# A three-block transformer on one core: row norms as fp32r products with ones, a T sum moved behind the output projection, and one whole block pair per feed-forward layer

## The chip, the core and the metric

The kernel runs on one core of one Trainium2 chip. The metric is the device time of one execution in microseconds (us), the median over several executions. The matmuls are done on TensorE (PE), elementwise work on VectorE (DVE), activations and copies on ScalarE (ACT), some additions and accumulating DMAs on GpSimd (POOL), and weight loads are issued by SyncE (SP).

## What is computed

The input is a sequence of 512 tokens of width 1024, in float32. Three layers follow each other. Each has a mixing part (mLSTM, banded attention, and a differential plus forgetting attention), an output projection that is added to x, and a feed-forward part. What matters here is the norms and the feed-forward part:

```
def rmsnorm(x, g):
    y = x * rsqrt(mean(x * x, axis=-1) + EPS)
    return y * g

def conv_ffn(h, w_up, conv_w, conv_b, w_down):   # layers 0 and 1
    u, g = split(h @ w_up)                       # 1024 -> 2 x 2816
    g = causal_dwconv(g, conv_w, conv_b)         # 3 taps along the tokens
    return (silu(g) * u) @ w_down

# layer 2 (second block): the same without the convolution, EPS 1e-5
# between layers 1 and 2: x = rmsnorm(rmsnorm(x, final_g), norm1_g_2) feeds the projections
```

## The kernel before

**Layout.** x lies in SBUF as X, transposed: 8 tiles k of 128 channels by 512 tokens. Every product is made of fp32r (a rounded float32) parts: an operand is split into a high part (H, by an ACT copy) and a low part (L, by a DVE subtraction), and three matmuls (WH with H, WH with L, WL with H) replace one. A group of 24 matmuls (8 k-steps of three) of 512 columns makes one tile of 128 outputs by 512 tokens.

**Order.** `order()` writes out one list of steps by hand. Each engine's function (`tensor`, `scalar`, `vector`, `gpsimd`) walks this one list and issues its own part of each step, so that each engine's queue is in the order of the list, and an instruction that waits holds up everything behind it on its engine. Semaphores connect the engines (`mark` and `at`). `conv_ahead` puts the weight splits (`conv` and `cconv`: WH by ACT at L1933 and L1944, WL by DVE at L2458 and L2480) as early as a slot of the four half-size weight slots is free.

**Norms.** Weights are applied to the unnormed x times g; the factor 1/rms of a token multiplies the result. The squares of X are summed into acc by POOL (L3183) or DVE. For `ffn0`, `ffn1`, `n2` and `kv` the steps `rstd_first` and `rstd_second` follow: PE sums acc over the partitions with 4 fp32 matmuls of one column (L1348), ACT takes the root of 128x4 values (L2082), DVE the inverse (L2662), PE spreads these with 4 fp32 matmuls of 128 columns (L1354), and ACT copies the spread rows to Rsb (L2103). The norm between layers 1 and 2 (`join_first`, `join_second`, `join_third`) does it for acc and for a second sum acc2.

**Feed-forward (`ffn_wino`).** 11 pairs of blocks of 256 hidden channels (gate and up). The first WHOLE[i] pairs, (2, 2, 1) for layers 0, 1 and 2, are done plainly: 4 tiles g, g, u, u of 24 matmuls each of 512 columns (L1460). The others use a Strassen-Winograd scheme, `wp`: 7 products of 24 matmuls each of 256 columns (L1793), PE's order q1, q5, q6, q3, q7, q2, q4, each with its own weight chunk of 128x1024, four of which are sums of blocks made by DVE (`wsum`, L2474). q1 and q6 share a PSUM bank: q6 waits until ACT has copied q1 out (`wcopy`, L2010). The products need sums of x as moving operands, the T sums: for each of four pairs p of k-tiles `wtB` (ACT, L1951), `wtS` (four DVE operations L2492 to L2503, then an ACT copy L1957 to TH) and `wtL` (DVE, L2510, to TL). In between stand the pieces of the down projection (`wd`, L1819), which are added to X by accumulating DMAs, and at the end its tail (`wtail`, L1842).

**Around the change.** Of the output projection, `out_rest` makes the tiles m = 0 to 7; after tile m the step `res_norm` adds it to X (DVE, L2917), makes hH of tile m (ACT, L2268), its square (ACT, L2276) and hL of tile m-1 (DVE, L2425); `res_last` makes hL of tile 7. `T_SUMS` names the T sums that stand behind an output tile: p = 0 behind tiles 4 and 5, and `wtB` of p = 1 behind tile 5. Where WHOLE is 1, `conv_ahead` (the chunks of q6 and q3), `wt0` twice (the conv taps on DVE, L2536, and silu on ACT, L1981; in layer 2 silu alone), `wy0`, then q1 with its `wcopy` stand in this order behind the last u tile. In layer 1 `fence acc2`, `gg` and `gate_weights C` stand between `res_last` and the first g tile: both ACT and DVE wait there for POOL's last square sum, and DVE waits for a small load.

Of the kernel before, what the change touches and what calls it, by code (L numbers as in the profile page):

```python
# [34 lines left out]
WHOLE = (2, 2, 1)  # L35
# [4 lines left out]
T_SUMS = {4: (("wtB", 0), ("wtS", 0)), 5: (("wtL", 0), ("wtB", 1))}  # L40
# [280 lines left out]
def pieces(hd):  # L321
# [3 lines left out]
    if hd % 2 == 0:  # L325
# [11 lines left out]
             "C": ([4, 5, 0, 1, 2, 3, 6, 7], 6)}  # L337
NEXT_NORM = {"A": "ffn0", "B": "ffn1", "C": "n2"}
# [8 lines left out]
def order():  # L347
# [5 lines left out]
    def put(*x):  # L353
        steps.append(x)
# [60 lines left out]
    def tile_done(*x):  # L415
# [13 lines left out]
        if norms:  # L429
            step = norms.pop(0)  # L430
            if step:
                put(*step)
                if step[0] == "join_second":
                    deferred.append(("join_third",))
# [154 lines left out]
    def ffn_wino(i, end):  # L589
# [404 lines left out]
def program(nc, wall, xt, memt, colsd, biasd, consts, rope, gatew, out):  # L994
    ctx = ExitStack()
    with ctx:
# [28 lines left out]
        K = place("K", [128, 5, 128])  # L1025
        KB = place("KB", [128, 3, 128], BF16)
        acc = place("acc", [128, 512])
        sq = [place(f"sq{i}", [128, 512]) for i in range(2)]
        diag = place("diag", [128, 512])
        held_w = place("held3", [128, 2, 256], offset=top[0] - 2048)  # L1030
# [108 lines left out]
        Tf = place("Tf", [128, 4, 256], offset=wino + 49152)  # L1139

# [169 lines left out]

        def normed(st, k):

            return ("hH", st, k), ("hL", st, k)
# [5 lines left out]
        def tensor(e):  # L1319
# [31 lines left out]

            def spread_column(o, c):

                return e.matmul(o, small[:, c:c + 1].broadcast_to([128, 128]), ident, start=True, stop=True)  # L1354

            def spread(what, b, before, key, c0=4):

                w.wait_ge(*at("rcol", "n1" if what == "join" else what))
# [19 lines left out]
            for what, *a in STEPS:  # L1378
# [85 lines left out]

                elif what == "tm":
# [73 lines left out]
                elif what == "rstd_rows":  # L1539
# [4 lines left out]
                    w.wait_ge(*at("acc" + SQ_LAST[a[0]], a[0], 7))  # L1544
                    e.matmul(ps[b][:, :], ones, acc[:, :], start=True, stop=True).then_inc(*mark("sums", a[0]))
# [5 lines left out]
                elif what == "join_first":  # L1551
                    b, before = bank(("rs", "join"), ("jsq", 0))
                    if before:
                        w.wait_ge(*at(*before))
                    w.wait_ge(*at("accD", "n1", 7))
                    sums(b, acc, 0, ("sums", "n1"))
                    w.wait_ge(*at("acc2", 7))
                    sums(b, acc2, 4, ("sums", "join"))

                elif what == "join_second":  # L1560
                    b, before = bank(("R", "n1"), ("Rsb", "n1"))
                    spread("n1", b, before, ("spread", "n1"))

                elif what == "join_third":
                    b, before = bank(("R", "join"), ("Rsb", "join"))
                    spread("join", b, before, ("spread", "join"), 32)
# [339 lines left out]
        def scalar(e):  # L1906
            w, mark = Lane(e), partial(ev.mark, "act")

            for what, *a in STEPS:
# [175 lines left out]
                elif what == "rstd_rows":  # L2085
# [7 lines left out]
                elif what == "last_sums":  # L2093
# [3 lines left out]
                                 bias=small[:, 61:62], scale=1.0 / 1024).then_inc(*mark("rsq", "last", h))  # L2097

# [249 lines left out]
                elif what == "join_first":  # L2348
                    w.wait_ge(*at("sums", "join"))
                    e.activation(small[:, 0:4], ps[BANK[("rs", "join")]][:, 0:4], ACT.Sqrt, bias=small[:, 60:61],  # L2350
                                 scale=1.0 / 1024).then_inc(*mark("rsq", "n1"))
                    w.wait_ge(*at("jsq", 1))
                    e.activation(small[:, 44:48], small[:, 40:44], ACT.Sqrt, bias=small[:, 61:62]).then_inc(
                        *mark("rsq", "join"))

                elif what == "join_second":
                    w.wait_ge(*at("spread", "n1"))
                    for x in R_USED["n1"]:
                        w.wait_ge(*at(*x))
                    e.activation(Rsb[:, :], ps[BANK[("R", "n1")]][:, :], ACT.Copy).then_inc(*mark("Rsb", "n1"))  # L2360

                elif what == "join_third":
                    w.wait_ge(*at("spread", "join"))
                    e.activation(acc2[:, :], ps[BANK[("R", "join")]][:, :], ACT.Copy).then_inc(*mark("Rsb", "join"))
# [17 lines left out]

                elif what == "lam_later":
                    w.wait_ge(*at("lamS"))
                    e.activation(small[:, 10:12], ps[BANK["lam"]][:, 0:2], ACT.Exp).then_inc(*mark("lamE"))
# [28 lines left out]
        def vector(e):  # L2414
# [8 lines left out]
            def low_part(st, k, g):  # L2423
# [3 lines left out]
                                       op1=ALU.subtract).then_inc(*mark("hL", st, k))  # L2427

# [13 lines left out]
            for what, *a in STEPS:  # L2442
# [76 lines left out]
                elif what == "wg0":  # L2519
# [3 lines left out]
                    w.wait_ge(*at("Rsb", FFN_NORM[i]))  # L2523
# [53 lines left out]
                elif what == "wgr":  # L2577
                    i, st = a
                    w.wait_ge(*at("Rsb", FFN_NORM[i]))
# [96 lines left out]
                elif what == "join_first":  # L2676
# [12 lines left out]
                    for x in RCOL_USED["n1"]:  # L2689
                        w.wait_ge(*at(*x))  # L2690
# [745 lines left out]
```

## Time and profile before

| | |
|---|---|
| three runs | 1775.87, 1775.97, 1776.04 us, median 1775.97 |
| profiled execution, own time | 1776.19 us |
| its span, first to last instruction | 1774.4 us |
| granted TensorE clock, mean | 0.999 |
| PE busy | 99% |
| DVE, ACT, POOL busy | 72%, 53%, 12% |

The profile is of one execution. The own time holds 1.8 us beside the span. In a timeline a row has start, duration, engine, line, operation, and in brackets how long its engine was idle before it and what released it; rows overlap a little, since an instruction begins before the one before it has ended. In the chain of work that ended last, a row has start, duration, engine and line of a piece.

### The profile page before, as it was taken

Reading aid. Unit: us, or ns where it says so; the run is one execution under the profiler, and the core shown is the slowest. Engines: PE = TensorE matmul, PEld = TensorE weight load, DVE = VectorE, ACT = ScalarE, POOL = GpSimd, SP = SyncE. Lnnn points to the kernel's source line nnn. Section 1 sums busy time; section 2 is a strip of 40 time slices with the busy share of each in tenths; the row PEclk is TensorE's granted clock in tenths of the full one; section 3 lists DMA queues with packets and bytes.
Section 4 is the critical chain, followed back from the end, with each engine's and each line's share of the span. In section 5 each row is a group of like instructions: output and inputs, shape, how many; then the busy total and the mean of one; then the engine's idle time right before and its main releaser. Section 6 shows DMA issues by size and latency. Waiting matters only on the chain.

```text
span 1774.4 us, 26361 instructions
## 1 busy us (share of the span) xinstructions
PE 1764.7 (99%) x10750; PEld 1533.1 (86%) x10750; DVE 1273.1 (72%) x1772; ACT 949.1 (53%) x1439; POOL 205.8 (12%) x225
## 2 busy tenths in 40 slices
PE   9999999999999999999999999999999999999998
PEld 7877788999999887777899999978777899999997
DVE  6878567788786655656888787687767487766766
ACT  6645444655555544755565555552567455454454
POOL 0001220110111200002011110103001101111110
PEclk9999999999999999999999999999999999999999
DMA  6231223654545343212364554443221235555442
GB/s 249 72 95 61 71 95 107 154 137 137 143 121 141 88 147 110 96 48 87 106 169 117 155 128 140 111 119 106 73 96 48 97 106 144 142 140 145 108 134 81
DMA packets 61623, 205.19 MB, mean 116 GB/s; under 512 B 7344, under 2 KB 9520, under 8 KB 53184
## 3 DMA queue, kind: packets, MB, share of 16 engines
q1 hardware_dynamic: 38832, 162.55, 27.7%
q0 software_dynamic: 17280, 31.46, 10.0%
q10 hardware_dynamic: 5392, 9.51, 1.7%
q8 instruction: 85, 1.39, 0.3%
q14 instruction: 34, 0.28, 0.0%
HBM read 169.38 MB, written 2.13 MB: 97 GB/s over the span
## 4 chain that ended last, share of the span: by engine, by line
PE 96%; DVE 2%; ACT 1%; DMA 0%; issue 0%; DVEq 0%; SPq 0%; ACTq 0%
PE ps L1793 31%; PE ps L1460 21%; PE ps L1819 16%; PE ps L1374 7%; PE ps L1479 4%; PE ps L1842 2%; PE ps L1499 2%; PE ps L1606 2%; PE ps L1651 2%; PE ps L1631 2%; PE ps L1690 1%; PE ps L1671 1%; PE ps L1860 1%; PE ps L1423 1%; DVE WL L2458 0%; PE ps L1354 0%
## 5 line engine op out<-in xcount | busy, mean ns | idle before, releaser
L1793 PE MATMUL ps<-hH,WL 128*128 128x256 f32 x896 | 253.6, 283 | 0.0
L1793 PE MATMUL ps<-hL,WH 128*128 128x256 f32 x896 | 253.6, 283 | 0.0
L1793 PE MATMUL ps<-hH,WH 128*128 128x256 f32 x896 | 253.4, 283 | 0.0
L2480 DVE TENSOR_TENSOR WL<-raw,WH 128x1024 fp32r<-128x1024 f32 x138 | 168.1, 1220 | 116.9 <-ACT WH L1944 116.9
L2458 DVE TENSOR_TENSOR WL<-raw,WH 128x1024 fp32r<-128x1024 f32 (+1 forms) x137 | 166.9, 1257 | 92.1 <-ACT WH L1933 91.8
L1460 PE MATMUL ps<-hH,WH 128*128 128x512 f32 x544 | 215.3, 396 | 0.0
L1460 PE MATMUL ps<-hH,WL 128*128 128x512 f32 x544 | 211.9, 390 | 0.0
L1460 PE MATMUL ps<-hL,WH 128*128 128x512 f32 x544 | 211.9, 390 | 0.0
L3207 POOL DMA_DIRECT2D X<-sq x120 | 104.8, 962 | 862.1 <-ACT sq L1999 860.2
L1793 PE MATMUL ps<-TH,WL 128*128 128x256 f32 x672 | 190.2, 283 | 0.0
L1793 PE MATMUL ps<-TL,WH 128*128 128x256 f32 x672 | 190.2, 283 | 0.0
L1793 PE MATMUL ps<-TH,WH 128*128 128x256 f32 x672 | 190.1, 283 | 0.0
L2480 DVE TENSOR_TENSOR WL<-Wsum,WH 128x1024 fp32r<-128x1024 f32 x112 | 136.7, 1221 | 69.2 <-ACT WH L1944 69.1
L1933 ACT ACTIVATE WH<-raw 128x1024 fp32r<-128x1024 f32 (+1 forms) x137 | 134.4, 1028 | 88.9 <-PE ps L1460 44.9
L1793 PEld LDWEIGHTS ps<-hL,WH 128*128 128x128 f32 x896 | 171.9, 192 | 1.2
L1793 PEld LDWEIGHTS ps<-hH,WH 128*128 128x128 f32 x896 | 171.9, 192 | 1.2
L1793 PEld LDWEIGHTS ps<-hH,WL 128*128 128x128 f32 x896 | 171.9, 192 | 0.0
L1819 PE MATMUL ps<-FH,WH 128*128 128x512 f32 x432 | 168.7, 391 | 0.0
L1819 PE MATMUL ps<-FL,WH 128*128 128x512 f32 x432 | 168.7, 390 | 0.0
L1819 PE MATMUL ps<-FH,WL 128*128 128x512 f32 x432 | 168.0, 389 | 0.0
L1944 ACT ACTIVATE WH<-raw 128x1024 fp32r<-128x1024 f32 x138 | 144.7, 1053 | 24.9 <-PE ps L1793 18.4
L1944 ACT ACTIVATE WH<-Wsum 128x1024 fp32r<-128x1024 f32 x112 | 118.0, 1054 | 55.9 <-PE ps L1793 42.6
(420 smaller groups left out, 3865.3 us busy)
## 6 DMA issues: line engine op xcount, KB each, us to landing
raw<-in_wall SPq DMA_DIRECT2D x166, 512.0 KB, 4.3
raw<-in_wall SPq DMA_DIRECT2D x65, 1024.0 KB, 4.9
X<-sq POOLq DMA_DIRECT2D x120, 256.0 KB, 4.0
bias<-in_bias ACTq DMA_DIRECT2D x12, 256.0 KB, 2.9
raw<-in_wall SPq DMA_DIRECT2D x8, 256.0 KB, 6.9
X<-in_xt SPq DMA_DIRECT2D x8, 256.0 KB, 7.7
CB<-rows ACTq DMA_DIRECT2D x8, 256.0 KB, 3.4
out_y<-X SPq DMA_DIRECT2D x8, 256.0 KB, 2.2
```

The lines of the kernel that those rows point to most:

```text
L1374: mm = e.matmul(ps[b][:, :], ww[:, k, c:c + 128], x, start=(k == seq[0] and i == 0), stop=(k == seq[-1] and i == 2))
L1460: mm = e.matmul(ps[b][:, 0:N], ww[:, k, c:c + 128], x[:, k, 0:N], start=(k == 0 and i == 0), stop=(k == 7 and i == 2))
L1479: mm = e.matmul(o, x[:, k, t * 128:t * 128 + 128], ww[:, k, :], start=(k == 0 and i == 0), stop=(k == 7 and i == 2))
L1499: mm = e.matmul(ps[b][:, :], x[:, k, t * 128:t * 128 + 128], ww[:, kx, :], start=(k == 0 and i == 0), stop=(k == 7 and i == 2))
L1606: mm = e.matmul(ps[b][:, c:c + L], queries[u["kind"]][r, u["m"], t * 128:t * 128 + 128], keys[u["kind"]][r, u["m"], 0:L], start=opens, sto ...
L1793: mm = e.matmul(ps[b][:, 256 * u:256 * u + 256], ww[:, p, 128 * u:128 * u + 128], x, start=(opens and p == 0 and u == 0 and n == 0), stop= ...
L1819: mm = e.matmul(ps[BANK["wd", i, g, m]][:, :], ww[:, kx, mi * 128:mi * 128 + 128], x[:, f % 8, :], start=(kx == 0 and n == 0), stop=(kx == ...
L1933: e.activation(WH[W_AT["unit", n] // 2][:, c], unit_raw(n)[:, c], ACT.Copy).then_inc(*mark("wh", n, x))
L1944: e.activation(chunk_slot(c)[0], chunk_src(c), ACT.Copy).then_inc(*mark("wh", "c", c))
L2458: e.tensor_tensor(WL[v][:, c], unit_raw(n)[:, c], WH[v][:, c].bitcast(F32), ALU.subtract).then_inc(*mark("wl", n, x))
L2480: e.tensor_tensor(L, chunk_src(c), H.bitcast(F32), ALU.subtract).then_inc(*mark("wl", "c", c))
L3207: e.dma_start(X[:, m, :], part[m % 2][:, :], accum_op=ALU.add).then_inc(s_part[m % 2], 16)
```

## The change

The four norms `ffn0`, `kv`, `ffn1`, `n2` and the one between layers 1 and 2 now go over whole rows. `row_split`: ACT copies acc to accH (fp32r) and DVE makes accL = acc - accH (128x512). `row_sums`: PE multiplies both with a 128x128 tile of ones (2 fp32r matmuls of 512 columns), ACT takes the root of 128x512 values into Rsb. `row_inverse`: DVE inverts Rsb (128x512). Where a column form is needed too (kv, n1), four DVE reductions pick it out. In the feed-forward layers `row_split` stands behind the first g tile, and the second g tile is cut in two halves of 12 matmuls with `row_sums` between them. The join makes both its sums before the first projection's second tile ends, with DVE also forming acc2 + 1e-5 acc. The T sum p = 1 (`wtS`, `wtL`) and `wtB` of p = 2 move from behind the first g tile to behind output tile 6. WHOLE becomes (1, 1, 1).

```
-WHOLE = (2, 2, 1)
+WHOLE = (1, 1, 1)
-T_SUMS = {4: (("wtB", 0), ("wtS", 0)), 5: (("wtL", 0), ("wtB", 1))}
+T_SUMS = {4: (("wtB", 0), ("wtS", 0)), 5: (("wtL", 0), ("wtB", 1)), 6: (("wtS", 1), ("wtL", 1), ("wtB", 2))}
...
     def rstd(i, eps):
-        norms.extend([None, ("rstd_rows", i, eps), None] if i in ("ffn0", "ffn1", "n2") else
-                     [None, ("rstd_first", i, eps), ("rstd_second", i)])
+        norms.extend([("row_split", i), ("row_sums", i, eps), ("row_inverse", i)])
...
+        def half(m, n, x):
+            put("fm_half", f"g{i}", m, n, 128 * (m % 2), st, x)
+
         n = take()
         whole("g", 0, n)
-        put("rstd_first", st, 61 if i == 2 else 60)
-        put("wtS", i, 1)
-        put("wtL", i, 1)
-        put("wtB", i, 2)
+        put("row_split", st)
+        half(1, n, 0)
+        put("row_sums", st, 61 if i == 2 else 60)
         put("wtS", i, 2)
-        whole("g", 1, n)
+        half(1, n, 1)
+        put("row_inverse", st)
         done.add(n)
-        put("rstd_second", st)
         if WHOLE[i] == 1:
             sum_ahead(i)
         put("wtL", i, 2)
...
-    norms.extend([None, ("join_first",), ("join_second",)])
+    norms.extend([None, ("join_sums",)])
     put("fence", "C")
     put("rope_load")
     put("chunk_bias")
+    put("join_split")
...
+            def row_sums(b, parts, key):
+
+                for n, x in enumerate(parts):
+                    mm = e.matmul(ps[b][:, :], ones_r[:, :], x[:, :], start=(n == 0), stop=(n == 1))
+                mm.then_inc(*mark(*key))
...
+                elif what == "row_sums":
 
                     b, before = bank(("rs", a[0]), ("rsq", a[0]))
                     if before:
                         w.wait_ge(*at(*before))
-                    w.wait_ge(*at("acc" + SQ_LAST[a[0]], a[0], 7))
-                    e.matmul(ps[b][:, :], ones, acc[:, :], start=True, stop=True).then_inc(*mark("sums", a[0]))
+                    w.wait_ge(*at("rowH", "ones"))
+                    w.wait_ge(*at("rowH", a[0]))
+                    w.wait_ge(*at("rowL", a[0]))
+                    row_sums(b, (accH, accL), ("sums", a[0]))
...
+                elif what == "row_split":
+                    w.wait_ge(*at("acc" + SQ_LAST[a[0]], a[0], 7))
+                    e.activation(accH[:, :], acc[:, :], ACT.Copy).then_inc(*mark("rowH", a[0]))
...
+            def row_low(low, whole, high, name):
+
+                w.wait_ge(*at("rowH", name))
+                e.tensor_tensor(low[:, :], whole[:, :], high[:, :].bitcast(F32), ALU.subtract).then_inc(
+                    *mark("rowL", name))
+
+            def row_columns(name):
+
+                for x in RCOL_USED[name]:
+                    w.wait_ge(*at(*x))
+                w.wait_ge(*at("rrow", name))
+                for i in range(4):
+                    c = slice(128 * i, 128 * i + 128)
+                    mark_i = mark("rcol", name) if i == 3 else mark("rcolh", name, i)
+                    e.tensor_tensor_reduce(diag[:, c], Rsb[:, c], ident, 1.0, 0.0, ALU.mult, ALU.add,
+                                           small[:, 4 + i:5 + i]).then_inc(*mark_i)
...
+                elif what == "row_inverse":
                     w.wait_ge(*at("rsq", a[0]))
                     e.reciprocal(Rsb[:, :], Rsb[:, :]).then_inc(*mark("rrow", a[0]))
+                    if a[0] == "kv":
+                        row_columns("kv")
...
+                elif what == "join_split":
+                    w.wait_ge(*at("acc2", 7))
+                    w.wait_ge(*at("accD", "n1", 7))
+                    e.scalar_tensor_tensor(out=acc2[:, :], in0=acc[:, :], scalar=1e-5, in1=acc2[:, :], op0=ALU.mult,
+                                           op1=ALU.add).then_inc(*mark("acc2", 8))
+                    row_low(accL, acc, accH, "join")
+                    row_low(acc2L, acc2, acc2H, "n1")
```

## Rows read from the trace of the kernel before

**Rows 1.** The page: part 1 (engine, busy us) and part 4 (the chain).

```profile
PE 1764.7 (99%) x10750; PEld 1533.1 (86%) x10750; DVE 1273.1 (72%) x1772; ACT 949.1 (53%) x1439; POOL 205.8 (12%) x225
...
PE 96%; DVE 2%; ACT 1%; DMA 0%; issue 0%; DVEq 0%; SPq 0%; ACTq 0%
```

**Rows 2.** The chain in order of time, layer 0: start, us, what.

```profile
265.95 0.79 PE ps L1348 x8
266.74 5.61 PE ps L1460 x24
272.34 0.89 PE ps L1354 x8
273.24 32.66 PE ps L1460 x144
```

**Rows 3.** The same chain: first g tile of the three layers, first products of layer 2.

```profile
260.51 5.44 PE ps L1460 x24
...
830.54 5.44 PE ps L1460 x24
...
1418.95 5.44 PE ps L1460 x24
...
1442.58 17.27 PE ps L1793 x144
```

**Rows 4.** The same chain at the join of layers 1 and 2.

```profile
1190.84 1.68 PE ps L1348 x16
...
1204.47 0.89 PE ps L1354 x8
```

**Rows 5.** Timeline of DVE, opening of layer 0.

```profile
259.30 0.74 DVE L2425 SCALAR_TENSOR_TENSOR hL<-X,cols,hH 128x512 fp32r<-128x512 f32 x1
260.55 0.69 DVE L2917 TENSOR_TENSOR X<-X,ps 128x512 f32<-128x512 f32 x1 [0.51 <-PE ps L1374]
261.15 2.08 DVE L2425 SCALAR_TENSOR_TENSOR hL<-X,cols,hH 128x512 fp32r<-128x512 f32 x2
...
267.17 0.47 DVE L2492 SCALAR_TENSOR_TENSOR Tf<-X,cols,Tf 128x256 f32<-128x256 f32 x1
...
269.86 0.96 DVE L2510 TENSOR_TENSOR TL<-Tf,TH 128x768 fp32r<-128x768 f32 x1 [0.91 <-ACT TH L1957]
```

**Rows 6.** Timeline of DVE, the last output tile's addition, layers 1 and 2.

```profile
831.11 0.68 DVE L2917 TENSOR_TENSOR X<-X,ps 128x512 f32<-128x512 f32 x1
...
1419.51 0.68 DVE L2917 TENSOR_TENSOR X<-X,ps 128x512 f32<-128x512 f32 x1
```

**Rows 7.** Timelines of ACT and POOL, opening of layer 0.

```profile
262.42 1.99 ACT L1933 ACTIVATE WH<-raw 128x1024 fp32r<-128x1024 f32 x2
...
262.59 1.80 POOL L3183 TENSOR_TENSOR acc<-acc,sq 128x512 f32<-128x512 f32 x1 [0.57 <-ACT sq L2276]
```

**Rows 8.** Timeline of DVE, opening of layer 1, what stands behind the fence.

```profile
835.40 0.17 DVE L2990 TENSOR_TENSOR gg<-cols 128x8 f32<-128x8 f32 x1 [1.25 <-POOL acc L3183]
...
837.17 0.23 DVE L2703 TENSOR_TENSOR gw<-graw,gg 128x64 f32<-128x64 f32 x1 [1.53 <-DMA graw<-in_gatew]
```

**Rows 9.** DVE: a group of instructions (busy us, mean ns), and the taps in the timeline.

```profile
L3078 DVE RECIPROCAL sq<-sq 128x512 f32<-128x512 f32 x1 | 3.3, 3346 | 0.0
...
301.19 2.98 DVE L2536 SCALAR_TENSOR_TENSOR yz<-gs,cols,yz 128x511 f32<-128x511 f32 x4 [0.29 <-ACT yz L1973]
```

**Rows 10.** Timeline of ACT, first products of layer 2.

```profile
1442.69 2.01 ACT L1944 ACTIVATE WH<-Wsum 128x1024 fp32r<-128x1024 f32 x2 [4.66 <-PE ps L1460]
...
1446.01 1.15 ACT L1981 ACTIVATE yz<-gs 128x512 f32<-128x512 f32 x2
1447.07 0.58 ACT L2010 ACTIVATE held<-ps 128x512 f32<-128x512 f32 x1
```

**Rows 11.** Timeline of DVE, first products of layer 2.

```profile
1446.19 1.22 DVE L2480 TENSOR_TENSOR WL<-Wsum,WH 128x1024 fp32r<-128x1024 f32 x1
```

**Rows 12.** Timeline of DVE, ahead of the kv norm.

```profile
616.61 2.36 DVE L2458 TENSOR_TENSOR WL<-raw,WH 128x1024 fp32r<-128x1024 f32 x2 [4.62 <-ACT WH L1933]
```

More of the change, by code:

```diff
@@ L337 @@
              "C": ([4, 5, 0, 1, 2, 3, 6, 7], 6)}
+ROW_NORMS = ("ffn0", "kv", "ffn1", "n2")
 NEXT_NORM = {"A": "ffn0", "B": "ffn1", "C": "n2"}
@@ L1029, in program @@
         diag = place("diag", [128, 512])
+        accH, accL = (place(f"acc{x}", [128, 512], F32R, offset=top[0] - 2048 * n) for x, n in (("H", 3), ("L", 2)))
         held_w = place("held3", [128, 2, 256], offset=top[0] - 2048)
@@ L1139, in program @@
         Tf = place("Tf", [128, 4, 256], offset=wino + 49152)
+        acc2H, acc2L = (place(f"acc2{x}", [128, 512], F32R, offset=wino + 81920 + 2048 * n)
+                        for n, x in enumerate("HL"))
         gw = place("gw", [128, 8, 32], offset=227840)
@@ L1309, in program, with r_ready @@
         BANK, FREED = {}, {}
+        def r_ready(name):
+            return ("rrow" if name in ROW_NORMS + ("n1", "join") else "Rsb"), name
         def normed(st, k):
@@ L1356, in spread @@
             def spread(what, b, before, key, c0=4):
-                w.wait_ge(*at("rcol", "n1" if what == "join" else what))
+                w.wait_ge(*at("rcol", what))
                 if before:
@@ L1463, in tensor @@
                     FREED["unit", n] = ("lin", name, m)
+                elif what == "fm_half":
+                    name, m, n, c, act, half = a
+                    W = weights(n, 8)
+                    if not half:
+                        b, before = bank((name, m), ("wg", name, m))
+                        if before:
+                            w.wait_ge(*at(*before))
+                    b = BANK[name, m]
+                    for k in range(4 * half, 4 * half + 4):
+                        w.wait_ge(*at(*weights_at(n, k)))
+                        for x in act_at(act, k):
+                            w.wait_ge(*at(*x))
+                        for i, (ww, x) in enumerate(((W[0], hH), (W[0], hL), (W[1], hH))):
+                            mm = e.matmul(ps[b][:, :], ww[:, k, c:c + 128], x[:, k, :],
+                                          start=(k == 0 and i == 0), stop=(k == 7 and i == 2))
+                    if half:
+                        mm.then_inc(*mark("lin", name, m))
+                        FREED["unit", n] = ("lin", name, m)
                 elif what == "tm":
@@ L1549, in tensor @@
                     spread(a[0], b, before, ("spread", a[0]))
[L1551 to L1566, printed above, removed]
+                elif what == "join_sums":
+                    for name, parts, drain in (("n1", (acc2H, acc2L), ("rsq", "n1")),
+                                               ("join", (accH, accL), ("rsq", "join"))):
+                        b, before = bank(("rs", name), drain)
+                        if before:
+                            w.wait_ge(*at(*before))
+                        w.wait_ge(*at("rowH", name))
+                        w.wait_ge(*at("rowL", name))
+                        row_sums(b, parts, ("sums", name))
                 elif what == "gates_later":
@@ L2346, in scalar @@
                             *mark("xg", m - 1, h))
[L2348 to L2357, printed above, removed]
+                elif what == "join_split":
+                    w.wait_ge(*at("accD", "n1", 7))
+                    e.activation(accH[:, :], acc[:, :], ACT.Copy).then_inc(*mark("rowH", "join"))
+                    w.wait_ge(*at("acc2", 8))
+                    e.activation(acc2H[:, :], acc2[:, :], ACT.Copy).then_inc(*mark("rowH", "n1"))
+                elif what == "join_sums":
+                    w.wait_ge(*at("sums", "n1"))
                     for x in R_USED["n1"]:
                         w.wait_ge(*at(*x))
[L2360 to L2364, printed above, removed]
+                    e.activation(Rsb[:, :], ps[BANK[("rs", "n1")]][:, :], ACT.Sqrt, bias=small[:, 63:64],
+                                 scale=1.0 / 1024).then_inc(*mark("rsq", "n1"))
+                    w.wait_ge(*at("sums", "join"))
+                    e.activation(acc2[:, :], ps[BANK[("rs", "join")]][:, :], ACT.Sqrt, bias=small[:, 60:61],
+                                 scale=1.0 / 1024).then_inc(*mark("rsq", "join"))
                 elif what == "bias":
@@ L3058, in vector @@
                     k = a[0]
-                    w.wait_ge(*at("Rsb", "join"))
+                    w.wait_ge(*at(*r_ready("join")))
                     w.wait_ge(*at("hL", "n1", k))
```

62 lines of the change are left out of this document (29 added, 33 removed).

## The prediction

> **What bounds the kernel now.** I read the page first, then the chain of work that ended last, then the timelines of DVE, ACT and POOL around each place that the change touches. The page has PE busy for 99% of the span, and the chain lies on PE for 96% [rows 1]. The reader is to see that PE has no slack to lose: what leaves PE's list is gained in full, and every wait put into PE's list is lost in full. The chain's pieces in layer 0 follow without a gap [rows 2]. DVE at 72% looks free, but it is not so in the openings of the feed-forward layers, where its queue is in order and almost full.
>
> **What PE saves.** A whole pair is four tiles of 24 matmuls of 512 columns; six such tiles take 32.66 us [rows 2], 5.44 each, so 21.77 a pair. The seven products that replace it take 24 matmuls of 256 columns each; 144 take 17.27 us [rows 3], 2.88 for 24, so 20.15. **Saved: 1.62 us in layer 0 and in layer 1**, 3.2 together. The eighth less of matmul columns is worth less than an eighth, since a short matmul costs 120 ns and half a long one 113.
>
> A norm's two fp32 pieces take 0.79 and 0.89 us, and the tile behind the first takes 5.61 where others take 5.44 [rows 2]; behind the second about 0.1 more is lost by the same step back from fp32 (an estimate from the first). That is 1.86 to 1.95; two fp32r matmuls of 512 columns cost 0.45. **Saved: 1.4 us at each of ffn0, kv, ffn1, n2**, 5.6 in all. At the join 1.68 + 0.17, then twice 0.89 [rows 4] (the other spread is alike), go, and four fp32r matmuls, 0.9, come: **2.75 saved**. In all PE is given 11.6 us. The other engines decide what is kept.
>
> **T sum p = 1 behind output tile 6.** On DVE these steps now stand ahead of the addition of tile 7. Rows 5 price them: from the first of the four operations (267.17) to the end of TL (270.82) they take 3.65 us, 0.91 of it waiting for ACT's copy. In layer 0 DVE is free of tile 6 at 260.0, so the addition of tile 7 starts at 263.6 in place of 260.55 [rows 5]. The last hL followed that addition's start by 2.7 us before; with POOL not yet adding I take 2.3. So hL of tile 7 is ready at 265.9. The first g tile begins at 260.51 [rows 3] and wants it for its eighth k-step, 21 matmuls or 4.76 us later, at 265.3: PE waits **0.7 us**. In layers 1 and 2 DVE had no idle time there, the addition moves from 831.11 and 1419.51 [rows 6] by the full 3.65, hL is there at 837.1 and 1425.5, and PE, which wants it at 835.3 and 1423.7 [rows 3], waits **1.8 us** in each. The bounds are 0, if DVE finds time for the block earlier, and 0.7 more in each layer, if hL follows by the 3 us that rows 5 nearly show.
>
> **The split of acc.** Before, the one-column sums waited for POOL alone. Now PE waits also for accL, and on DVE that stands behind the weight split of the first u unit, which itself waits for ACT's WH. The square of tile 7 is late by what the addition is late. In layer 0 ACT's WH, 1.99 us for two [rows 7], now runs from 265.5 to 267.5, DVE's WL ends at about 269.2, accL at 269.9; POOL's add (1.80 [rows 7]) is done before. PE reaches the sums after half a g tile, at 265.95 + 0.7 + 2.72 = 269.4, and waits **0.5 us**; the same in layer 2. In layer 1 a fence comes between: DVE passed it at 835.40 and was at the gate weights at 837.17 [rows 8]. The square sum is late by the 3.65 of the addition, less some 0.5 that POOL's add gains where DVE idles beside it (an estimate), so the gate weights are at 840.2, WL ends at 842.6 and accL at 843.2. PE is there at 835.98 + 1.8 + 2.72 = 840.5 and waits **2.7 us**. At kv the WL of a unit ends at 618.97 [rows 12], accL 0.65 later, at 619.6; the sums stood at 618.5: **1.1 us**. At the join accH and accL fit into the second projection tile (ends at 1189.7 by my count, sums at 1190.7); only the first gate product then waits about 0.4 us for Rsb, behind a 3.3 us inverse.
>
> **The inverse of 128x512.** It costs DVE 3.35 us [rows 9] in place of 0.18, six times in all. It is covered in the feed-forward openings by the two u tiles (10.9 us of PE): I count DVE's queue from accL (269.9): T sum 2, inverse, two weight sums, T sum 3, two WL, two gs, 14.4 us, so 284.3; the last u tile ends at 284.0. The first product's WL is made by 281.9. So it costs nothing by itself, but all the slack is used, and the next part pays.
>
> **The pair itself: taps ahead of q1's copy.** In layer 2, which already has one whole pair, ACT makes WH of q6 and q3 (1442.69), silu of both tiles, and then copies q1 out at 1447.07 to 1447.65 [rows 10]. PE starts q1 at 1442.58 [rows 3] and wants that copy for q6, two products or 5.76 us later, at 1448.34. It holds by 0.7 us. In layers 0 and 1 there are also the conv taps, four DVE operations, 2.98 us [rows 9], which stand behind the WL of q3; silu of the second tile waits for them, and q1's copy waits behind silu on ACT. With DVE as early as in layer 2, WL of q3 ends 4.83 us after q1's start [rows 3, 11]; taps 2.9, silu 0.6 [rows 10], copy 0.6: 8.95, less 5.76 is a wait of 3.2 us. With the queue as counted above (WL of q3 at 289.5, taps to 292.4, silu 293.1, copy 293.6, PE due at 289.7) it is **3.9 us in layer 0 and in layer 1**. I take this, since the inverse is in that queue. After it every later need is 3.9 us later too, and I find none late: q7's T sum is ready at 295.8 and wanted at 299.4. In layer 2 the 0.7 shrinks to some 0.4, and nothing is paid.
>
> **The sum.** Layer 0: -1.4 + 0.7 + 0.5 - 1.6 + 3.9 = +2.1. Layer 1: -1.4 + 1.8 + 2.7 - 1.6 + 3.9 = +5.4. Layer 2: -1.4 + 1.8 + 0.5 = +0.9. kv: -0.3. Join: -2.75 + 0.4 = -2.35. Together +5.8 us. The profiled execution took 1776.19, so 1782.0; it stands 0.2 above the median, so **1781.8** as a median. With the hL wait and the copy wait at their lower ends (0 and 3.2) and accL's waits halved it is some 8 less, with their upper ends some 3 more.
>
> **Rivals.** *The copy wait does not come*, because ACT's copy is early enough or the taps find DVE idle, and the rest holds: 7.8 less, 1774.0, no change that can be told. For it speaks that layer 2's opening runs clean; against it, that layer 2 has no taps and just 0.7 us to spare [rows 10]. *All waits are hidden*: the full 11.6 is kept, 1764.4. This is the other side. It is decided at one place, the in-order DVE queue: if its delay behind output tile 6 stays below what PE has in hand (265.3 less 263.23, about 2.1 us, in layer 0), the first wait goes, and only if taps and silu end before q6 does the second. For it speaks PE's unbroken run before; against it 3.65 us of inserted work [rows 5] and the taps' 2.98. *DVE falls further behind*: POOL's adds stretch its rows (two hL took 2.08 in place of 1.5 [rows 5]), or a weight chunk comes late behind the inverse: 1 us more in each opening, 1785. *The clock falls* after a wait: if the 24 matmuls behind each of the two long waits ran at half rate, each would cost 2.88 us more [rows 3], 1787.6. For it speaks nothing in the trace: the mean granted clock is 0.999, the higher of the two levels, but the chain has no wait of PE of such a length [rows 2], so the trace does not speak strongly against it either. By the Trainium skill, page "TensorE: Matmul & The Clock Gate", section "HAM oscillation — how this bites in real kernels", a tensor engine that waits too long between bursts of matmuls drops to the lower clock and must earn the higher one back; by that rule this rival's time would hold, without it the forecast's.
>
> **How the numbers follow.** Forecast 0.60; copy wait absent 0.11; all hidden 0.14; DVE further behind 0.10; clock 0.05. A measurement of this kernel can tell about 0.2%, 3.55 us, from no change, so above 1779.5 is slower and below 1772.4 faster. The forecast's own range is 1778.5 to 1784.8, of which a little lies within the 0.2%. Faster 0.14, same 0.14, slower 0.72. The range reaches from below the first rival, 1773, to the clock rival, 1787; left out is mainly the case in which all is hidden.
>
> **What would show it.** In the changed kernel: a wait of PE before q6 of the first product group in layers 0 and 1 on ACT's held copy, near 4 us each, and none in layer 2; a wait of the first g tile on hL in all three layers, 1.8 in two; a wait of the row sums on accL, longest in layer 1; the gap between the two g tiles at 0.45 us where none of these bite. It would be wrong if PE's rows ran through these four kinds of place without idle time, or if the held copy of q1 lay ahead of silu on ACT.

## The result, and the profile after

| | before | after |
|---|---|---|
| median of the runs | 1776.01 us (4 runs, 1775.87 to 1776.17) | 1788.53 us (4 runs, 1787.30 to 1789.66) |
| profiled execution, own time | 1776.19 us | 1787.87 us |
| its span | 1774.4 us | 1786.1 us |

The ratio is 1.0070, 95% interval 1.0058 to 1.0082: **12.5 us slower**, where 5.8 were forecast. The profiled execution is 11.7 us longer, and the working below is against it.

The page of the kernel after, parts 1 and 4, for [rows 1]:

```profile
PE 1761.6 (99%) x10810; PEld 1534.1 (86%) x10810; DVE 1315.5 (74%) x1810; ACT 960.9 (54%) x1452; POOL 204.4 (11%) x226
...
PE 89%; DVE 6%; ACT 3%; issue 1%; DMA 0%; POOL 0%; DVEq 0%; SPq 0%; ACTq 0%
```

PE is busy for 3.1 us less, and yet the span is 11.7 longer; the chain, 96% PE before, now spends 9% on DVE and ACT. What PE waits for (engine and line, releaser; us in total, times, longest):

```profile
PE ps L1826 <- ACT held L2043: 7.3, 2, 3.7
PE ps L1477 <- ACT hH L2310: 6.8, 3, 2.6
...
PE ps L1366 <- DVE accL L2468: 1.3, 2, 1.0
```

None of the three rows was there before. They are the three waits of the forecast: q6 for the copy of q1, the first g tile for the parts of h, the row sums for accL.

**The first g tile.** Timeline of DVE, opening of layer 0, for [rows 5]:

```profile
260.48 1.56 DVE L2552 SCALAR_TENSOR_TENSOR Tf<-X,small,Tf 128x256 f32<-128x256 f32 x1
262.07 0.48 DVE L2556 SCALAR_TENSOR_TENSOR Tf<-X,small,Tf 128x256 f32<-128x256 f32 x1
263.46 0.96 DVE L2563 TENSOR_TENSOR TL<-Tf,TH 128x768 fp32r<-128x768 f32 x1 [0.91 <-ACT TH L1990]
264.34 0.68 DVE L2974 TENSOR_TENSOR X<-X,ps 128x512 f32<-128x512 f32 x1
264.94 1.62 DVE L2461 SCALAR_TENSOR_TENSOR hL<-X,cols,hH 128x512 fp32r<-128x512 f32 x2
```

and of PE beside it:

```profile
263.92 0.39 PE L1477 MATMUL ps<-hH,WL 128*128 128x512 f32 x1
265.83 0.47 PE L1477 MATMUL ps<-hH,WH 128*128 128x512 f32 x1 [1.51 <-ACT hH L2310]
```

PE stops after 18 matmuls, at the seventh k-step, not the eighth: the last row of DVE is two hL, those of tile 6 and of tile 7, and both stand behind the addition of tile 7. (The profile puts the wait down to ACT's hH of tile 7, which ended at about the same time, but this k-step takes its operands from tile 6 alone; in run 7 the profile names DVE's hL.) That addition is at 264.34 (forecast 263.6), since one of the moved operations took 1.56 us instead of 0.48, beside an addition of POOL that began at 260.46 and took 1.29; the same operation took 1.55 in layers 1 and 2. By the Trainium skill, page "SBUF — State Buffer", section "SBUF: two separate sides", DVE instructions with two SBUF inputs and POOL's exclude each other from a shared pair of ports for a whole instruction; the stretched row agrees. No run moves POOL's addition away. From its first matmul to the next tile's the first g tile takes 7.41 us (260.07 to 267.48) instead of 5.44, and it takes 3.23 and 3.15 us too much in layers 1 and 2.

**The copy of q1.** Timeline of DVE in layer 0, the taps of [rows 9]:

```profile
290.22 2.98 DVE L2589 SCALAR_TENSOR_TENSOR yz<-gs,cols,yz 128x511 f32<-128x511 f32 x4
```

ACT behind it, for [rows 10]:

```profile
293.23 0.63 ACT L2014 ACTIVATE yz<-yz 128x512 f32<-128x512 f32 x1 [0.81 <-DVE yz L2589]
293.77 0.58 ACT L2043 ACTIVATE held<-ps 128x512 f32<-128x512 f32 x1
```

and PE, layers 0 and 1:

```profile
294.40 0.38 PE L1826 MATMUL ps<-TH,WH 128*128 128x256 f32 x1 [3.64 <-ACT held L2043]
...
870.96 0.39 PE L1826 MATMUL ps<-TH,WH 128*128 128x256 f32 x1 [3.66 <-ACT held L2043]
```

Taps, silu, copy, q6, as forecast, with 3.64 and 3.66 us of idle time for 3.9. Layer 2 has no such row.

**The clock.** PE in stretches (from, to; length, busy (matmuls), granted clock, DMA share, GB/s): layer 0 around q6, layer 1 around the wait in the first g tile and behind it:

```profile
285.00:294.00 9.00, 5.76 (x49) 1.00 0.35 118
294.00:299.00 5.00, 4.60 (x26) 0.66 0.00 0
296.00:298.00 2.00, 2.00 (x11) 0.50 0.00 0
299.00:304.00 5.00, 5.00 (x44) 1.00 0.37 105
837.00:841.00 4.00, 1.36 (x6) 1.00 0.02 7
841.00:846.00 5.00, 5.00 (x16) 0.66 0.03 7
```

In this execution, 1.0 to 1.6 us after PE resumes, the granted clock falls from 1.00 to 0.50, from the 2.4 to the 1.2 GHz level, for 3.4 us. This happens four times in the profiled execution: behind both copy waits, and behind the waits of 2.6 us in layers 1 and 2, but not behind the 1.5 us in layer 0. (It falls once more in the last microseconds, where PE has almost nothing left to do, in every profiled execution, that of the kernel before too; this is left out below.) In the chain, layer 2, the two halves of the second g tile:

```profile
1435.79 4.24 PE ps L1496 x12
1440.48 2.72 PE ps L1496 x12
```

The first half costs 1.52 us more for the same 12 matmuls. The q6 behind the copy wait took 4.47 us (294.40 to 298.87) for 2.88.

**The join** is as forecast: 1177.84 to 1206.31 before, 1188.63 to 1214.77 after, 2.3 us less.

### The profile page after: what moved, and what is told of

The parts are those of the page before. It is cut to its first block, busy times and chain, and to the rows that moved or that the text cites. A ratio compares the mean times of both kernels' runs of the same rounds, so it can differ in the third digit from the quotient of the medians.

```text
span 1786.1 us, 26556 instructions
## 1 busy us (share of the span) xinstructions
PE 1761.6 (99%) x10810; PEld 1534.1 (86%) x10810; DVE 1315.5 (74%) x1810; ACT 960.9 (54%) x1452; POOL 204.4 (11%) x226
## 4 chain that ended last, share of the span: by engine, by line
PE 89%; DVE 6%; ACT 3%; issue 1%; DMA 0%; POOL 0%; DVEq 0%; SPq 0%; ACTq 0%
PE ps L1826 33%; PE ps L1852 17%; PE ps L1477 16%; PE ps L1516 4%; PE ps L1391 3%; PE ps L1875 3%; PE ps L1639 2%; PE ps L1536 2%; PE ps L1684 2%; PE ps L1664 2%; DVE WL L2511 2%; PE ps L1723 1%; ACT hH L2310 1%; PE ps L1704 1%; ACT WH L1966 1%; PE ps L1893 1%
## 5 line engine op out<-in xcount | busy, mean ns | idle before, releaser
L1826 PE MATMUL ps<-hL,WH 128*128 128x256 f32 x960 | 271.8, 283 | 0.0
L1826 PE MATMUL ps<-hH,WL 128*128 128x256 f32 x960 | 271.7, 283 | 0.0
L1826 PE MATMUL ps<-hH,WH 128*128 128x256 f32 x960 | 271.6, 283 | 0.0
L1826 PE MATMUL ps<-TH,WH 128*128 128x256 f32 x720 | 205.0, 285 | 7.3 <-ACT held L2043 7.3
L1826 PE MATMUL ps<-TH,WL 128*128 128x256 f32 x720 | 205.1, 285 | 0.0
L1826 PE MATMUL ps<-TL,WH 128*128 128x256 f32 x720 | 205.1, 285 | 0.0
L1477 PE MATMUL ps<-hH,WH 128*128 128x512 f32 x456 | 180.5, 396 | 6.8 <-ACT hH L2310 6.8
L1826 PEld LDWEIGHTS ps<-hH,WH 128*128 128x128 f32 x960 | 184.4, 192 | 1.2
L1477 PE MATMUL ps<-hH,WL 128*128 128x512 f32 x456 | 177.9, 390 | 0.0
L1477 PE MATMUL ps<-hL,WH 128*128 128x512 f32 x456 | 177.7, 390 | 0.0
```

The costliest lines, as they stand in the source:

```text
L1477: mm = e.matmul(ps[b][:, 0:N], ww[:, k, c:c + 128], x[:, k, 0:N], start=(k == 0 and i == 0), stop=(k == 7 and i == 2))
L1826: mm = e.matmul(ps[b][:, 256 * u:256 * u + 256], ww[:, p, 128 * u:128 * u + 128], x, start=(opens and p == 0 and u == 0 and n == 0), stop= ...
```

## The experiments

Fifteen kernels, each with a profile and five or eleven timed runs, beside runs of the kernel before on the same chip (medians 1775.8 to 1776.2). Where edits shift lines, the same code has slightly other line numbers.

**1. The pair undone.** `-WHOLE = (1, 1, 1)` `+WHOLE = (2, 2, 1)`.

> The changed kernel with WHOLE back at (2, 2, 1), nothing else undone. Theory: each of layers 0 and 1 has lost 3.65 us to PE's wait for the copy of q1 and some 1.55 us more in the q6 product behind it, where the granted clock was down to its lower level for about 3.4 us, against 1.62 us gained by the pair; so the pair alone costs 2 x 3.6 = 7.2 us, and this kernel is at 1788.5 - 7.2 = 1781.3 us, with no wait and no fall of the clock at q6 in layers 0 and 1, and with the waits of the first g tiles on hH and hL as they are. Rival 1 (the fall of the clock has another cause than the wait ahead of it): 1788.5 - 4.1 = 1784.4. Rival 2 (the DVE queue is the bound in the openings, and its delay comes out at another place of the two whole pairs): above 1785.

Measured 1783.03 us, ratio 1.0041 (1.0028 to 1.0053): 5.5 less than the whole change, and between the theory's 1781.3 and the first rival's 1784.4, so the time alone doesn't decide between them. The waits for q1's copy are gone, and part of what this gives goes to accL, whose waits are 3.1 us longer in all (4.4 for 1.3). The profiled execution has no fall of the clock at all, although the first g tiles wait as before:

```profile
PE ps L1477 <- ACT hH L2310: 6.8, 3, 2.7
PE ps L1366 <- DVE accL L2468: 4.4, 4, 2.7
```

So the same wait of 2.6 us lowers the clock in one execution and not in another, and where it doesn't, PE is early at the sums and waits there: accL comes when DVE makes it. In that execution the accL waits are 0.3, 2.7, 0.3 and 1.2 at kv, within 0.2 of the forecast's 0.5, 2.7, 0.5 and 1.1.

**2. The T sum undone** (`wtS` 1, `wtL` 1, `wtB` 2 behind the row sums).

> The changed kernel with the T sum p = 1 and the wtB of p = 2 back behind the first g tile (here behind the row sums). Theory: the waits of PE in the first g tile (1.5, 2.6 and 2.6 us of idle time, with two steps of about 0.15 us more in each) go, and with them the two falls of the clock behind the longer ones (1.5 us each): 10 us less at those places. DVE has to do the 3.65 us of work after the sums instead, with 1 to 3 us of it uncovered in front of the first product or of q1's copy in each of layers 0 and 1: 1778.5 if nothing of it is uncovered, 1784 if 3 us are in both. Rival (the block behind tile 6 isn't what delays hH and hL): the waits in the first g tile stay, 1788.5 or above.

Measured 1787.56, ratio 1.0066 (1.0053 to 1.0079): hardly faster, and 3.6 above the upper end of the theory. The waits in the first g tile are gone, and DVE pays the same work at the copy:

```profile
PE ps L1829 <- ACT held L2046: 13.1, 3, 5.9
PE ps L1829 <- DVE WL L2536: 2.1, 2, 1.1
PE ps L1369 <- DVE accL L2471: 1.8, 1, 1.8
```

The clock is lower for longer, too: in this execution for 6.8, 3.4 and 6.8 us, 17 in all, where it was 13.7 in the change. The 3.4 us stand behind a wait of only 1.81 us, in layer 1:

```profile
844.41 0.47 PE L1369 MATMUL ps<-accH,ones_r 128*128 128x512 f32 x1 [1.81 <-DVE accL L2471]
845.00:849.00 4.00, 4.00 (x12) 0.57 0.67 252
```

**3. q1's copy ahead of taps and silu.**

```
+put("wp", i, 1, 1)
+put("wcopy", i, 1, 1)
 for m in (0, 1):
     put("wt0", f"g{i}", m)
```

> The changed kernel with one edit of order: q1 of the first product pair and its copy stand ahead of the conv taps and silu in the list, so that ACT copies q1 out as soon as it is done and only then does silu; PE's own order is the same. Theory (the wait at q6 is ACT's order and nothing else): the two waits of 3.65 us and the falls of the clock behind them (1.55 us each) go, 1788.5 - 10.4 = 1778.1, with no new wait. Rival 1 (the wait is DVE's lateness, and the next thing that needs the taps or silu is late instead): a wait of the same size appears at q7, the first down piece or a T sum, 1785 to 1788.5. Rival 2 (the clock falls by themselves): 1788.5 - 7.3 = 1781.2.

Measured 1784.83 (1783.95 to 1787.41), ratio 1.0051 (1.0039 to 1.0064), 6.7 above the theory. The profiled execution is the slowest of the five, 1787.41, with the clock lower for 6.8 us in layer 1. The wait moved on by one copy, to q5's, which still stood behind silu and the high part of T7. Timeline of ACT, layer 0:

```profile
293.14 0.63 ACT L2018 ACTIVATE yz<-yz 128x512 f32<-128x512 f32 x1 [0.81 <-DVE yz L2593]
293.68 1.04 ACT L2000 ACTIVATE hH<-T7f 128x1024 fp32r<-128x1024 f32 x1
294.63 1.04 ACT L1981 ACTIVATE WH<-Wsum 128x1024 fp32r<-128x1024 f32 x1
295.57 0.57 ACT L2047 ACTIVATE held<-ps 128x512 f32<-128x512 f32 x1
```

and of PE, at q3:

```profile
296.20 0.38 PE L1830 MATMUL ps<-hH,WH 128*128 128x256 f32 x1 [2.69 <-ACT held L2047]
```

**4. Matmuls in the waits**, to tell clock from wait:

```
+def idle(count):    # into the next free bank
+    for n in range(count): e.matmul(ps[b], ones_r, ones_r broadcast to 4x128)
+idle(6)     ahead of k = 6 of the first g tile
+idle(12)    ahead of q6 of the first product pair, layers 0 and 1
```

> The changed kernel with matmuls that compute nothing put where PE waits: 12 of 128x512 (ones by ones, into a bank not in use; about 0.23 us each, 2.7 us) ahead of the wait for q1's copy in layers 0 and 1, and 6 (1.4 us) ahead of the seventh k-step of the first g tile in all three layers. They are shorter than the waits, so what comes next starts when it started before. Theory (the clock falls because PE stands still): no fall behind the five waits, the first q6 takes 2.88 us and not 4.47, and the time is 1788.5 - 4 x 1.55 = 1782.3 us. Rival (the clock falls for another cause, or my 1.55 us are something else): 1788.5. A third (the extra matmuls delay the tiles): above 1788.5.

Measured 1784.14 (1783.68 to 1784.84), ratio 1.0047 (1.0033 to 1.0060). PE, layer 1:

```profile
835.90 1.52 PE L1375 MATMUL ps<-ones_r 128*128 128x512 f32 x6
838.74 0.47 PE L1489 MATMUL ps<-hH,WH 128*128 128x512 f32 x1 [1.32 <-ACT hH L2324]
```

and the stretches that had the falls:

```profile
842.00:846.00 4.00, 1.41 (x7) 1.00 0.02 4
...
873.00:877.00 4.00, 4.00 (x36) 1.00 0.29 71
```

No fall is left, though what PE needs comes no earlier: the falls come from PE standing still. **4.4 us of the 12.5 are the clock.** Not the 6.2 that the four falls take, because accL's wait in layer 1 grew from 1.0 to 2.6: there a slow PE only filled a wait.

**5. Each part alone.** The norms alone are the change with both other edits undone; the other two are the kernel before with one line of constants changed (and the moved steps taken from their old place).

> The change with the pair and the T sum both undone: only the five norms as in the changed kernel. Theory (the price that the prediction put on the norms): 1.4 us less at each of the four norms and 2.3 less at the join, against waits for accL of 1.8 us in layer 1 and 1.1 us at kv: 1776.0 - 5.6 - 2.3 + 2.9 = 1771.0 us, up to 1774 if kv's opening also waits for hH as it did in the run with the pair undone (1.2 us) and layers 0 and 2 wait 0.3 to 0.5 each. Rival (the inverse of 128x512 holds up DVE's queue in the layers' openings): above 1776, with waits of PE on WL or held.

> The kernel before with only the T sum p = 1 and wtB of p = 2 behind output tile 6; the norms and the two plain pairs as they were. Theory: PE waits in the seventh k-step of the first g tile, 1.5 us in layer 0 and 2.6 in layers 1 and 2, and about 0.15 more in each on the next step: 7.3 us, 1783.3; each fall of the granted clock behind one of the two longer waits adds 1.5 to 1.7, so up to 1786.5. Rival (the waits need the new norms, whose split stands in the same queues): at most 2 us, 1778.

> The kernel before with only WHOLE = (1, 1, 1). Theory (DVE's queue bounds the opening; its inverse of 3.35 us isn't in it here, and the T sum p = 1 is): in the run with the T sum undone PE waited 5.9 us for q1's copy and 1.0 for a WL in layer 0; less 3.2 for the inverse, a wait of 3.7 us is left in each of layers 0 and 1, with a fall of the clock (1.6 us) behind it, less 1.6 saved: 2 x 3.7 = 7.4 us more, 1783.4. Rival 1 (the inverse is what makes the copy late): the wait is below 1 us, and the time 1776 - 3.2 + 2 = 1774.8 or less. Rival 2 (it isn't DVE's queue but the taps' place alone): a wait of 3.65 and no wait on WL at all, the same time, 1783.

| alone | us | ratio |
|---|---|---|
| norms | 1775.33 (1774.25 to 1778.69) | 0.9998 (0.9989 to 1.0007) |
| T sum | 1788.64 (1788.38 to 1788.86) | 1.0070 (1.0057 to 1.0082) |
| pair | 1784.12 (1782.96 to 1784.76) | 1.0043 (1.0030 to 1.0055) |

The T sum alone costs as much as the whole change, the pair two thirds of that: 0.8 us less, 12.5 and 8.0 more make 19.7, not 12.5. They share DVE's queue, and the work moved ahead of the addition is work less in front of the copy: PE waits 13.1 us for copies in run 2, which has the pair without the moved T sum, and 7.3 in the change. The T sum's time is 2.1 above the range expected, which run 6 takes up. The norms came out above the 1771 to 1774 expected: layer 2 gave its gain back, at q1's WL (1.10 us) and at the copy (1.43), and accL was late by 1.8 in layer 1 and 1.2 at kv.

**6. The T sum alone, with 6 matmuls in the wait.**

> The kernel before with only the T sum moved, as in the run of that part alone (1788.6 us), and 6 matmuls of 128x512 that compute nothing ahead of the seventh k-step of the first g tile, shorter than the wait there. Theory (of the 12.6 us that the moved T sum costs by itself some 7.3 to 8 are waits and the rest is the clock, down for 6.8 us in layer 2 in the profiled run and at least as long in the others): no fall, 1784 us. Rival (the rest is something else): 1788.6.

Measured 1785.01 (1784.86 to 1785.09), ratio 1.0051 (1.0038 to 1.0063): 3.6 us less than without them, with the extra matmuls the only edit, so this much is the clock. In the profiled run without them layer 2 had a long fall:

```profile
1433.00:1437.00 4.00, 4.00 (x15) 0.50 0.19 20
```

and with them none:

```profile
1433.00:1437.00 4.00, 4.00 (x23) 1.00 0.25 72
```

**7. Half of the T sum moved** (`6: (("wtS", 1),)`, and `wtL` 1, `wtB` 2 behind `res_last`).

> The changed kernel with only the first half of the moved T sum (the four Tf operations and ACT's copy) behind output tile 6, and its TL and the wtB of p = 2 behind hL of tile 7. Theory (PE waits in the seventh k-step for hL of tile 6, which stands behind the addition of tile 7, and this behind the whole moved block): the addition starts 1.8 us earlier (the 0.91 us wait for TH and the 0.96 of TL are off its way), so the wait of layer 0 goes, 2.8 us become about 0.8 in layers 1 and 2, too short to lower the clock; in layer 1 the wait for accL grows from 1.0 to 3.0, since it ends with DVE and POOL and not with PE. Together 1788.5 - 1.7 - 2 x 2.0 - 2 x 1.5 + 2.0 = 1781.8. Rival (the wait is for tile 7's parts, in the eighth step, as the prediction had it): the waits vanish in all three layers, 1779.5. Rival 2 (what is delayed is the square sum, not hL): no change, 1788.5.

Measured 1786.43 (1785.04 to 1786.83). In the first g tiles the waits are those of the theory, none in layer 0 and this in layer 1, so it is the seventh k-step and hL of tile 6:

```profile
837.54 0.47 PE L1483 MATMUL ps<-hH,WH 128*128 128x512 f32 x1 [0.77 <-DVE hL L2467]
845.47 0.77 PE L1372 MATMUL ps<-accH,ones_r 128*128 128x512 f32 x1 [3.24 <-DVE accL L2474]
```

The total was missed by 4.6: accL was late by 1.2 also in layers 0 and 2 (DVE has the TL to make first), and the clock fell again, from the end of the 3.2 us for accL on and behind both copy waits.

**8. The copies of q1 and q5 both early.**

> The changed kernel with q1 and its copy and also q5 and its copy ahead of taps and silu in the list. With only q1's copy ahead, the wait moved by one product: q3 waited 2.7 us for q5's copy, which stood behind silu and the seventh T's high part. Theory (DVE's queue is nearly the bound here, and ACT's order costs only what lies between): q5's copy is early, and the next thing late is the WL of q7, made at 297.4 us in layer 0 where PE wants it at 296.4: a wait of about 1 us in each layer, too short to lower the clock; against the changed kernel 2 x (5.2 - 1.0) = 8.4 us less, 1780.1. Rival (the copies were the only thing late): no wait, 1778. Rival 2 (the wait moves on again at full size): 1784 or above.

Measured 1784.19, ratio 1.0045 (1.0033 to 1.0058), 4.1 above the theory. WL of q7 is late by 1.07 as said; what I had not seen is FL, 0.9 late at the first down piece, and both in layer 2 too, which had no wait there before. So the early copies cost layer 2 some 2 us.

**9. The pair on top of a repaired order** (edits of run 10 below, WHOLE (1, 1, 1)).

> The first repaired version with WHOLE back at (1, 1, 1), so with all three layers in the order of the changed kernel but the T sum back behind the first g tile, accL early and the copies of q1 and q5 ahead of silu. Theory (in layers 0 and 1 DVE's queue between the first g tile and the WL of q7 is longer than PE's work in it, by 2.3 us as the changed kernel's rows add up, and 0.9 more at the first down piece): 2 x (3.2 - 1.6) = 3.2 us above the first repaired version, 1775.3. Rival (with ACT's order mended the pair keeps its gain): 3.2 us below it, 1768.9.

Measured 1784.21, ratio 1.0046 (1.0034 to 1.0059). Run 10 took 1776.39, so the pair costs 7.8 us, not 3.2, with the clock down for 6.8 us in each of layers 0 and 1. In the openings PE waits on DVE alone:

```profile
PE ps L1835 <- DVE WL L2542: 12.5, 6, 3.4
PE ps L1861 <- DVE FL L2690: 1.8, 2, 0.9
```

**10 and 11. The norms repaired**: `row_split` ahead of the next unit's weight split, the early copies in layer 2 (10), and at kv the row sums a tile later (11).

> The five norms without the pair and without the moved T sum, with two repairs of what the norms-only run showed: accH and accL are made ahead of the next unit's weight split in the three layers (there 1.8 us of wait in layer 1), and in layer 2 q1, q5 and their copies stand ahead of silu (there 1.4 us of wait). Theory (PE's list is shorter by 1.4 us at each norm and 2.1 at the join, and waits of PE are all that takes from it): 1775.3 - 1.8 - 1.4 = 1772.1 us, with the waits of 1.2 at kv and 1.1 at layer 2's first WL left. Rival (the split ahead makes the weight split late, and PE waits in the u tiles): 1775 or above.

> The run before it with one more edit: at kv the row sums stand one tile later, since accL was late by 1.2 us behind the second tile. Theory: that wait goes and nothing takes its place, 1770.9 us. Rival (the later inverse holds up the tiles' drains and a bank is late): 1772 or above.

Measured 1776.39 and 1776.46, ratios 1.0004 (0.9995 to 1.0012) and 1.0003 (0.9994 to 1.0011): no gain, where 1772.1 and 1770.9 were expected. Yet at the start of layer 2 the profiled execution of run 11 is 5.5 us ahead of the kernel before; layer 2's opening gives 5.0 back:

```profile
PE ps L1835 <- DVE WL L2542: 3.4, 2, 2.3
...
PE ps L1861 <- DVE FL L2690: 0.9, 1, 0.9
```

With 0.3 for a copy these waits are 4.6 us, where the norms alone had 2.5: here too the early copies cost layer 2 some 2 us, as in run 8. The clock takes about 1.5 more, in run 11's execution and not in run 10's behind the same wait of 2.31 us:

```profile
1437.98 0.36 PE L1835 MATMUL ps<-hH,WH 128*128 128x256 f32 x1 [2.31 <-DVE WL L2542]
1439.00:1443.00 4.00, 4.00 (x23) 0.57 0.02 4
```

**12. Layer 2's inverse cut to a quarter**, on the norms alone. It leaves the root of three quarters of the tokens uninverted in that norm.

> The norms-only run with layer 2's inverse cut to a quarter: 128x128 in place of 128x512, so three quarters of the tokens of that layer's norm stay uninverted. Theory (the 1.1 us of wait for q1's WL and the 1.4 us for its copy in layer 2 come from the 3.35 us of the inverse in DVE's queue): 2.5 us less than with norms only, 1775.3 - 2.5 = 1772.8, and neither wait is there. Rival (they come from accL or from ACT's order): 1775.3, waits as they were.

Measured 1772.60 (1770.78 to 1774.02), ratio 0.9980 (0.9971 to 0.9989), 2.7 less than the norms alone. The wait for q1's WL is gone, that for the copy 0.38. So it is the inverse, 3.35 us, that DVE has no room for in layer 2.

**13. The version to keep.** Run 11 with layer 2's own norm by columns, as in the kernel before, and no early copies.

```
 WHOLE (2, 2, 1), T_SUMS as before
+row_split ahead of the first unit's weight split, layers 0 and 1
+norms.extend([("row_split", i)] + [None] * (i == "kv") + ...)
+layer 2: rstd_first, rstd_second, and not row_split, row_sums, row_inverse
```

> As the repaired version with kv's sums one tile later, but layer 2's own norm by columns as in the kernel before (and its copies in their old place). In that version the profiled run stood 5.5 us ahead of the kernel before when layer 2 began, and gave back 5.0 in layer 2's opening: 2.3 and 1.0 us of wait for a WL, 0.9 for FL, and the fall of the clock behind them. Theory (the 128x512 inverse and the early copies put DVE's queue over PE's work there, and only there): the 5.5 us are kept, 1776.0 - 5.5 = 1770.5. Rival (layer 2's loss is the T sum's place or another part of the change): 1773 or above.

Measured **1770.19** (1770.11 to 1771.36), ratio 0.9969 (0.9956 to 0.9981): 0.3 from the 1770.5 expected, 6.0 us faster than the kernel before, 18 faster than the change. Of the waits that the kernel before lacked these are left:

```profile
PE ps L1914 <- DVE Gf L2466: 0.6, 1, 0.6
...
PE ps L1837 <- ACT held L2054: 0.4, 1, 0.4
```

## Why the prediction was wrong

It had the sign, the places and most of the mechanisms, but not the clock; the size was out, and 1788.5 lies above the range's end of 1787.0. Term by term, in the profiled execution after (us over the whole kernel; a term of the copy is the idle time alone, the others are all that the stretch took too long):

| term | forecast | measured |
|---|---|---|
| PE's list shorter | -11.6 | about -11.6 |
| first g tile waits for hL | 0.7 + 1.8 + 1.8 = 4.3 | 2.0 + 3.1 + 3.1 = 8.2 |
| sums wait for accL (with kv) | 0.5 + 2.7 + 0.5 + 1.1 = 4.8 | 0.5 + 1.1 + 0 + 0 = 1.6 |
| q6 waits for the copy | 3.9 + 3.9 = 7.8 | 3.65 + 3.65 = 7.3 |
| join waits for Rsb, Gf | 0.4 | 0.6 |
| lower clock | 0 | 1.6 + 1.6 + 1.5 + 1.5 = 6.2 |
| sum | 5.8 (as the layers were rounded) | 12.3 (span: 11.7) |

**PE's saving** is not measured by itself: the last row's 12.3 against 11.7 is how well it closes. The parts seen alone fit: 2.3 at the join for 2.35; in run 13, from the start of the first g tile to the end of the plain pairs in layer 0, 1.4 (43.97 for 45.38) for 1.4.

**The failed step is the clock**, "For it speaks nothing in the trace", at 0.05. The trace before had no wait of PE of that length, so it could speak neither way; two waits of nearly 4 us were in my own sum. Run 4 puts 4.4 us on it; without them the change would be at 1784.1, inside the range. The section of the Trainium skill's page "TensorE: Matmul & The Clock Gate" that the prediction named, "HAM oscillation — how this bites in real kernels", has it right that waits between matmuls bring the lower clock; the four falls agree. The gap that it gives as its rule is longer than the waits of 2.6 us here and the 1.81 of run 2; the measurement decides. My price for it was also off: 24 matmuls at half rate, 2.88 us, for each of two waits; it was 3.4 us at half rate, some 1.55 lost, and behind the 2.6 us waits too.

**The hL wait**: the step "wants it for its eighth k-step, 21 matmuls" took hL of tile 7 as the late one. hL of tile 6 stands behind the same addition and is wanted three matmuls, 0.7 us, earlier (run 7). The addition itself was 0.7 us later than said (264.34 for 263.6), with one DVE operation stretched beside POOL's addition by 1.1, which the prediction had only as a rival.

**The accL wait** was right in size for a PE at full clock (run 1); after, the later and slower PE used it up. At kv it was 0, against 1.2 in run 1; PE came there 3.4 us later than in run 1 (611.92 for 608.47) and DVE's accL only 0.3 later (621.25 for 620.98). The traces show what held DVE in run 1 and not in the change, an accumulating DMA into X ahead of the opening:

```profile
597.90 1.29 DVE L3019 TENSOR_TENSOR X<-X,ps 128x512 f32<-128x512 f32 x2 [3.75 <-DMA X<-sq]
```

In the change the same additions begin at 597.44 without such a wait, although POOL issued that DMA 4.2 us later (590.95 for 586.72). Why it landed so much sooner was not tried. The errors of the hL and accL terms, +3.9 and -3.2, nearly cancel, in part by luck, and that is why clock and total miss by about the same.

**The copy wait** held, 3.65 for 3.9, with layer 2 free of it. But the cause is deeper than "q1's copy waits behind silu on ACT": with the order mended (runs 3, 8, 9) the wait turns up at the next thing that DVE makes. DVE's queue in the opening is longer than PE's work in it, so the pair pays in none of the orders tried; and "it costs nothing by itself" of the inverse is true only while other waits hold PE back (run 12).

**The rival "all waits are hidden"** fell at both of its points: the moved block delayed the addition by more than 2.1 us, and behind taps and silu the copy was 3.65 us late for q6.

## What to carry to other kernels

Where PE is full, count the queue of the engine that feeds it from the opening's first instruction to its last: if that sum is over PE's, moving a step ahead or behind mostly chooses the place of the wait, as runs 2, 3 and 8 did here. Put a price on the clock too for waits of PE like the 2.6 and 3.65 us here, about 1.5 us each, unless another wait stands right behind. And try the parts of a change by themselves: here the norms, 0.8 us by themselves, held a gain of 6 us (0.3%) once their own waits were mended, which the other two parts hid.

## What the runs showed that I had not expected

- The same wait lowers the clock in some executions and not in others (run 1 against the change). In the profiled executions, counted over the openings of the feed-forward layers, all 11 waits of 3.1 us and more had a fall, 9 of the 14 between 2.59 and 2.69 us, one of three near 2.3 (run 11), one of three near 1.8 (run 2), and none of 1.5 us or less. A fall lasted 3.4 us or 6.8 (run 6: 15 matmuls in 4 us for 23). What decides between them was not tried.
- Runs of one kernel can lie further apart than those of the kernel before (1.0 us over 15 runs): 4.4 us for the norms alone and 3.2 for run 12, over 11 runs each, but 0.5 for the T sum alone. Falls may be the cause, since the longest waits of the first two are 1.8 us, like the one that had a fall in run 2; their profiled executions have none, so this is not shown.
- Extra matmuls in a wait made a kernel faster (runs 4 and 6, by 4.4 and 3.6 us), with no work taken away.
